# Expert loop of a two-block model: VectorE alone makes the low halves of the weight tiles, and the gated units are split ahead of them

## The chip, the core and the metric

The program runs on one core of one Trainium2 chip. The time is the device time of one execution in microseconds (us), as a median over runs. The core has five engines with queues of their own: TensorE (PE, with its weight loads shown apart as PEld), VectorE (DVE), ScalarE (ACT), GpSimd (POOL) and SyncE (SP), which only issues DMAs here. They meet at semaphores: an instruction waits until a counter has reached a value, and a finished instruction raises one.

## What is computed

Two models are applied in a row to 256 tokens of width 1024 in fp32: a first block of two layers (convolution and state-space mixers, adaptive norms, and a mixture of experts), and a second block of four layers with plain feed-forward parts. The part that the change touches is the mixture of experts of the first block, which runs once a layer:

```python
def hier_moe(h, p):            # top-1 expert group, then top-2 SwiGLU experts inside it
    ...
    def expert(acc, ew):
        wg, wu, wd, cw = ew
        hid = jax.nn.silu(t @ wg) * (t @ wu)
        return acc + (cw[:, None] * (hid @ wd)).astype(acc.dtype), None
    out, _ = lax.scan(expert, jnp.zeros(t.shape, jnp.float32),
                      (p["w_gate"], p["w_up"], p["w_down"], comb))
```

There are 16 experts with 256 hidden units each.

## The kernel before

**Three products for one.** Every large fp32 product is made of three products in a reduced fp32 format (`mm3`, lines 655 to 659): high part times high part, low part times high part, high part times low part. So each weight tile that a DMA brings into `ring` (four buffers of 128x2048) needs a high part, which ACT rounds off into one of two buffers `high` (`make_high`, L1212), and a low part, tile minus high part, written over the tile itself (`make_low`, L371). The down tiles (`dring`, 128x1024) have the same pair in L1218 (`make_down_high`) and L378 (`make_down_low`). `shared(c)` says for each tile whether its low part is cut in two: then DVE makes columns 0 to 1023 and POOL 1024 to 2047, with a semaphore each (`low_dve`, `low_pool`), and TensorE waits for both in `low_ready` (L355). Of the down tiles, DVE and POOL always make 512 columns each.

**The expert loop.** Tokens have been sorted into blocks of 128 rows, one block `b` for each expert, and each expert is two slices `j` of 128 hidden units. So a layer's loop has 16 blocks, 32 slices, in a hardware loop of four slices a turn. An even slice `j` and the odd one after it form a pair. The engines' queues, in the order of one slice (`one(j, g)` in each `experts`):

- TensorE: in an even slice turn the rows of the next block (L895, eight transposes); gate and up product of tile j+1, first half (12 matmuls of L657 to L659); turn the hidden units of slice j (L912, waits for `hid_raw`); second half of the product; the down product of slice j (six matmuls, waits for the down tile's low parts and for `hidden`). Each half of the gate and up product waits for the tile's low parts **and** for `x_split`, the low part of the block's rows. So the first product of a block, which TensorE makes in the odd slice before it, needs tile and rows of that block ready.
- ACT: SiLU of the gate (L1407, `gate_act`); high part of weight tile j+2 (L1212, 128x2048); high part of the turned hidden units (L1411, `hid_high`); in an even slice the high part of the next block's rows (L1389, two instructions); high part of down tile j+1 (L1218); in an odd slice, once the down product is done, copy the block's result out (L1398, two instructions) and store it (L1403).
- DVE: hidden units = SiLU times up (L1976, `hid_raw`); low part of weight tile j+2, its half (L371); low part of the hidden units (L1980, `hidden`); in an even slice the low part of the next block's rows (L1971, two instructions, then `x_split`); low part of down tile j+1, its half (L378).
- POOL: in an even slice the load of the rows of a later block (L540); its halves of weight tile j+2 (L371) and of down tile j+1 (L378).

Ahead of the loop stands the router (L1862 on), a chain of small DVE instructions; DVE and POOL make the low part of the layer's second expert tile just before it (`tiles(("rt", l))`). A second loop for experts with over 128 tokens (`over`) is skipped at run time here.

## Time and profile before

| | us |
|---|---|
| median of 3 runs | 2782.28 |
| lowest and highest of the 3 | 2775.22, 2788.04 |
| span of the profiled execution | 2783.9 |
| PE busy over the span | 2328.6 (84%) |
| DVE busy | 1625.2 (58%) |
| POOL busy | 1323.9 (48%) |
| ACT busy | 1104.4 (40%) |

The profiled execution is one execution, and its span stands 1.6 us above the median of the three runs. The two expert loops lie at about 524 to 712 us and at 1063 to 1260 us of it, some 385 us together. Busy times of the whole span mix stages with quite different limits, so the loops are read by themselves. In a timeline row the first number is the start in us from the span's start, the second the duration in us; a row "x2" is two instructions in a row; the bracket tells how long the engine had been idle and what ended that.

### The profile page before, as it was taken

The page shows a single profiled execution, that of the slowest core. Times are in us where ns is not written, and L with a number is a line of the kernel's source. Part 1 is how long each engine was busy: PE and PEld are TensorE (multiplying, and loading weights), DVE is VectorE, ACT ScalarE, POOL GpSimd, SP SyncE. Part 2 cuts the span into 40 slices and gives each one's busy share as a digit, 9 for nine tenths or more (in the row PEclk, how much of TensorE's full clock was granted, in tenths as well). Part 3 has the DMA queues.
Part 4 walks back from the last instruction along what each step waited for, and adds up shares of the span by engine and source line. Part 5 has one row for each costly group of instructions (what it writes and reads, how often), then busy time and mean ns, then how long its engine had stood idle before and what let it go on. Part 6 is the DMA issues. An engine that isn't in the chain of part 4 may idle for free.

```text
span 2783.9 us, 41385 instructions
## 1 busy us (share of the span) xinstructions
PE 2328.6 (84%) x15250; PEld 1960.5 (70%) x15250; DVE 1625.2 (58%) x2522; ACT 1104.4 (40%) x1581; POOL 1323.9 (48%) x744
## 2 busy tenths in 40 slices
PE   5998777788498767785999997768999799999998
PEld 2864545677385466674868995325899699887998
DVE  3488464477558545674247555996555755523654
ACT  3222533466433435764434442001443344444443
POOL 2320132588442336882654552874565256441553
PEclk7995888899797888997989998668999899999999
DMA  5258602699326037883405441001455244342442
GB/s 228 91 202 322 217 15 91 228 341 344 144 96 252 1 112 268 321 296 133 171 24 199 186 172 71 0 0 52 165 192 189 91 181 182 135 152 91 152 181 91
DMA packets 93047, 443.73 MB, mean 159 GB/s; under 512 B 9088, under 2 KB 25600, under 8 KB 56704
## 3 DMA queue, kind: packets, MB, share of 16 engines
q1 hardware_dynamic: 79104, 390.10, 38.6%
q0 software_dynamic: 8496, 31.99, 3.0%
q10 hardware_dynamic: 5328, 20.04, 1.8%
q8 instruction: 77, 1.26, 0.2%
q14 instruction: 42, 0.34, 0.0%
HBM read 401.20 MB, written 40.89 MB: 159 GB/s over the span
## 4 chain that ended last, share of the span: by engine, by line
PE 40%; DVE 5%; POOL 3%; ACT 2%; DVEq 2%; POOLq 1%; issue 1%; DMA 0%; ACTq 0%
PE bank L657 11%; PE bank L658 11%; PE bank L659 11%; POOL ring_halves L371 2%; PE bank L699 2%; ACT high L1212 1%; PE bank L1123 1%; POOLq L593 1%; DVEq L2179 1%; PE bank L1061 1%; DVE HT L1633 1%; POOLq L598 1%; PE bank L1038 1%; DVE rstd L1618 1%; PE bank L1051 1%
## 5 line engine op out<-in xcount | busy, mean ns | idle before, releaser
L371 POOL TENSOR_TENSOR ring_halves<-ring,high 128x1024 fp32r<-128x1024 f32 (+1 forms) x230 | 814.2, 3541 | 953.9 <-ACT high L1212 953.9
L657 PE MATMUL bank<-ssdb_halves,high 128*128 128x256 f32 (+1 forms) x2080 | 619.6, 298 | 65.8 <-DVE HT_halves L1627 34.8
L658 PE MATMUL bank<-HT_halves,high 128*128 128x256 f32 (+1 forms) x2096 | 627.4, 299 | 0.0
L659 PE MATMUL bank<-ssdb_halves,ring_halves 128*128 128x256 f32 (+1 forms) x2080 | 615.5, 296 | 0.0
L1212 ACT CAST high<-ring 128x2048 fp32r<-128x2048 f32 x230 | 438.0, 1906 | 89.7 <-PE bank L659 89.7
L657 PEld LDWEIGHTS bank<-ssdb_halves,high 128*128 128x128 f32 x2080 | 400.8, 193 | 90.5 <-issue 61.2
L371 DVE TENSOR_TENSOR ring_halves<-ring,high 128x1024 fp32r<-128x1024 f32 x200 | 279.5, 1398 | 248.0 <-ACT high L1212 247.9
L658 PEld LDWEIGHTS bank<-HT_halves,high 128*128 128x128 f32 x2096 | 402.6, 192 | 8.9
L659 PEld LDWEIGHTS bank<-ssdb_halves,ring_halves 128*128 128x128 f32 x2080 | 398.4, 192 | 9.6
L378 DVE TENSOR_TENSOR dring_halves<-dring,dhigh 128x512 fp32r<-128x512 f32 x152 | 309.6, 2037 | 53.1 <-ACT dhigh L1218 53.0
L378 POOL TENSOR_TENSOR dring_halves<-dring,dhigh 128x512 fp32r<-128x512 f32 x152 | 264.5, 1740 | 80.7 <-ACT dhigh L1218 80.6
L657 PE MATMUL bank<-border_halves,dhigh 128*128 128x256 f32 x704 | 197.5, 281 | 0.0
L659 PE MATMUL bank<-border_halves,dring_halves 128*128 128x256 f32 x704 | 197.3, 280 | 0.0
L658 PE MATMUL bank<-border_halves,dhigh 128*128 128x256 f32 x704 | 197.3, 280 | 0.0
L1218 ACT CAST dhigh<-dring 128x1024 fp32r<-128x1024 f32 x152 | 160.8, 1058 | 54.2 <-PE bank L659 54.1
L659 PE MATMUL bank<-high,HT_halves 128*128 128x256 f32 x640 | 182.0, 284 | 0.0
L1456 ACT ACTIVATE border<-bank 128x256 f32<-128x256 f32 x88 | 33.8, 384 | 365.0 <-PE bank L659 365.0
L657 PE MATMUL bank<-high,HT_halves 128*128 128x256 f32 x512 | 156.8, 306 | 18.0 <-POOL ring_halves L371 11.0
L2017 DVE TENSOR_TENSOR border<-border,bank 128x256 f32<-128x256 f32 x88 | 37.1, 422 | 213.9 <-ACT border L1456 213.1
L1123 PE MATMUL bank<-wide,zs_b 128*32 128x256 f32 x256 | 96.7, 547 | 62.5 <-DVE wide L2190 62.5
L658 PE MATMUL bank<-ring_halves,HT_halves 128*128 128x256 f32 x512 | 145.5, 284 | 0.0
L657 PEld LDWEIGHTS bank<-border_halves,dhigh 128*128 128x128 f32 x704 | 132.6, 188 | 0.1
(415 smaller groups left out, 4603.3 us busy)
## 6 DMA issues: line engine op xcount, KB each, us to landing
ring<-in_ffn SPq DMA_DIRECT2D x88, 1024.0 KB, 5.4
ring<-in_moe SPq DMA_DIRECT2D x64, 1024.0 KB, 7.3
ring<-in_ada SPq DMA_DIRECT2D x48, 1024.0 KB, 6.9
dring<-in_ffn_down SPq DMA_DIRECT2D x88, 512.0 KB, 3.6
dring<-in_moe_down SPq DMA_DIRECT2D x64, 512.0 KB, 4.6
ring<-in_foxin SPq DMA_DIRECT2D x24, 1024.0 KB, 4.8
ring<-in_win SPq DMA_DIRECT2D x22, 1024.0 KB, 4.8
zs_b<-x_slots POOLq DMA_DIRECT2D x32, 512.0 KB, 8.8
```

Of the source, the lines that this page charges most:

```text
L371: eng.tensor_tensor(low, w, h, ALU.subtract).then_inc(sem(f"low_{engine}"), 1)
L378: eng.tensor_tensor(low, w, h, ALU.subtract).then_inc(sem(f"down_low_{engine}"), 1)
L593: pool.drain()
L657: mm(o, a[0], b[0], start=first, stop=last and bool(kw), **kw)
L658: mm(o, a[0], b[1], start=False, stop=last and bool(kw), **kw)
L659: return mm(o, a[1], b[0], start=False, stop=last, **kw)
L699: i = mm(ps[7][:, 0:tok.stop - tok.start], k("mean1024"), sq[:, c, tok], start=c == 0, stop=c == KC - 1)
L1123: i = mm(y, cT[:, part, j, :], z, start=False, stop=n == 3, skip_group_check=True, tile_position=(0, q))
L1212: nc.scalar.copy(r(high[c % HIGH][:]), ring[t % RING][:]).then_inc(sem("high"), 1)
L1218: nc.scalar.copy(r(dhigh[d % HIGH][:]), dring[d % RING][:]).then_inc(sem("down_high"), 1)
L1456: act_fn(gact[:, j % 2, :], ps[4 + j % 2][:, 0:T], ACT.Silu).then_inc(sem("gate_act"), 1)
L2017: tt(hraw, gact[:, j % 2, :], ps[4 + j % 2][:, T:2 * T], ALU.mult)
```

## The change

Tiles are sorted into three kinds. `LOW_POOL` (win, wout): POOL alone, as before. `LOW_BOTH` (the feed-forward, attention and S5 weights): both engines, half each, as before. All others, which are the router's tile and the expert tiles (rt, moe, over), and the experts' down tiles: DVE alone, 2048 and 1024 columns in one instruction. `CUT[c]` is the column up to which DVE works, and `LOWS` and `DOWN_LOWS` count each engine's tiles so that the waits of TensorE name the right value. POOL's part of the expert loop keeps only the loads of rows. And in DVE's slice, the low part of the hidden units comes directly behind the product that makes them, ahead of the weight tile.

```diff
-WITH_DVE = ("rt", "moe", "over", "ffn", "foxin", "foxf", "foxout", "s5in", "glu")
+LOW_POOL = ("win", "wout")
+LOW_BOTH = ("ffn", "foxin", "foxf", "foxout", "s5in", "glu")
...
-            SHARED.append((SHARED[-1] if SHARED else 0) + (_n[0] in WITH_DVE))
+            CUT.append(0 if _n[0] in LOW_POOL else TILE // 2 if _n[0] in LOW_BOTH else TILE)
+            for _e, _own in (("dve", CUT[-1] > 0), ("pool", CUT[-1] < TILE)):
+                LOWS[_e].append((LOWS[_e][-1] if LOWS[_e] else 0) + _own)
...
         def low_ready(c, g=0):
 
-            if shared(c):
-                nc.tensor.wait_ge(sem("low_dve"), SHARED[c] + RING * g)
-            nc.tensor.wait_ge(sem("low_pool"), c + 1 + RING * g)
+            if CUT[c] > 0:
+                nc.tensor.wait_ge(sem("low_dve"), LOWS["dve"][c] + RING * g)
+            if CUT[c] < TILE:
+                nc.tensor.wait_ge(sem("low_pool"), LOWS["pool"][c] + RING * g)
...
         def make_low(eng, engine, c, g=0):
 
-            if engine == "dve" and not shared(c):
+            at_ = slice(0, CUT[c]) if engine == "dve" else slice(CUT[c], TILE)
+            if at_.start == at_.stop:
                 return
-            cut = TILE // 2 if shared(c) else 0
-            at_ = slice(0, cut) if engine == "dve" else slice(cut, TILE)
...
         def make_down_low(eng, engine, d, g=0):
-            at_ = slice(0, D // 2) if engine == "dve" else slice(D // 2, D)
+            at_ = slice(0, DOWN_CUT[d]) if engine == "dve" else slice(DOWN_CUT[d], D)
+            if at_.start == at_.stop:
+                return
...
                         rows(j // 2 + 2, g)
-                    if j + 2 < slices:
-                        make_low(pool, "pool", c0 + j + 2, g)
-                    if j + 1 < slices:
-                        make_down_low(pool, "pool", d0 + j + 1, g)
...
                     tt(hrows[:, j % 2, :], gact[:, j % 2, 0:P], ps[4 + j % 2][:, P:TCOLS], ALU.mult).then_inc(sem("hid_raw"), 1)
-                    if j + 2 < slices:
-                        make_low(dve, "dve", c0 + j + 2, g)
                     dve.wait_ge(sem("hid_high"), hid_high0 + j + 1 + RING * g)
                     tt(r(hid[:, j % 2, 1, 0:P]), ps[4 + j % 2][:, TCOLS:TCOLS + P], hid[:, j % 2, 0, 0:P], ALU.subtract)\
                         .then_inc(sem("hidden"), 1)
+                    if j + 2 < slices:
+                        make_low(dve, "dve", c0 + j + 2, g)
```

DVE's queue in an even slice of the expert loop, before. The names are output<-inputs; `ring_halves` is the tile's low part, `border_halves` the low part of the hidden units, `HT_halves` that of the rows, `dring_halves` that of the down tile.

```order
L1976 TENSOR_TENSOR border<-border,bank 128x128 [waits gate_act]
L369 REGISTER_ALU
L371 TENSOR_TENSOR ring_halves<-ring,high 128x1024 [waits high]
L1980 TENSOR_TENSOR border_halves<-bank,border_halves 128x128 [waits hid_high]
L1968 REGISTER_ALU
L1971 TENSOR_TENSOR HT_halves<-bank,HT_halves 128x512 [waits x_high]
L1971 TENSOR_TENSOR HT_halves<-bank,HT_halves 128x512
L376 REGISTER_ALU
L378 TENSOR_TENSOR dring_halves<-dring,dhigh 128x512 [waits down_high]
```

The same slice in the changed kernel, whose lines are numbered a little differently (L1974, L1976, L376, L1969 and L385 are what L1976, L1980, L371, L1971 and L378 were):

```order
L1974 TENSOR_TENSOR border<-border,bank 128x128 [waits gate_act]
L1976 TENSOR_TENSOR border_halves<-bank,border_halves 128x128 [waits hid_high]
L374 REGISTER_ALU
L376 TENSOR_TENSOR ring_halves<-ring,high 128x2048 [waits high]
L1966 REGISTER_ALU
L1969 TENSOR_TENSOR HT_halves<-bank,HT_halves 128x512 [waits x_high]
L1969 TENSOR_TENSOR HT_halves<-bank,HT_halves 128x512
L383 REGISTER_ALU
L385 TENSOR_TENSOR dring_halves<-dring,dhigh 128x1024 [waits down_high]
```

The split of the hidden units has moved ahead of the weight tile, and weight and down tile have doubled in columns; the rows' split stands behind the weight tile in both.

POOL's queue in the same even slice, before:

```order
L544 REGISTER_ALU
L540 ISA [waits x_turned]
L540 DMA zs_b<-x_slots 128x1024
L369 REGISTER_ALU
L371 TENSOR_TENSOR ring_halves<-ring,high 128x1024 [waits high]
L376 REGISTER_ALU
L378 TENSOR_TENSOR dring_halves<-dring,dhigh 128x512 [waits down_high]
```

And in the changed kernel, up to the end of the loop's turn:

```order
L551 REGISTER_ALU
L547 ISA [waits x_turned]
L547 DMA zs_b<-x_slots 128x1024
L393 REGISTER_ALU
L393 COMPARE_AND_BRANCH
```

Both low parts have left the queue, so a load of rows now waits for nothing but the buffer (`x_turned`) and the load before it.

## Rows read from the trace of the kernel before

**Rows 1.** Busy times by stretch: window, us, each engine (instructions), clock, DMA share, GB/s.
```profile
540.00:700.00 160.00, 135.62 (x915) 118.03 (x913) 119.98 (x132) 110.72 (x158) 139.60 (x66) 1.00 0.93 338
1075.00:1243.00 168.00, 134.93 (x915) 117.85 (x914) 118.53 (x130) 117.38 (x164) 138.97 (x66) 1.00 0.91 325
```

**Rows 2.** Waits from 540 to 700 us: who waited for whom, us, times, longest.
```profile
PE bank L657 <- DVE border_halves L1980: 16.3, 13, 1.3
...
PE bank L657 <- POOL ring_halves L371: 4.9, 12, 0.4
```

**Rows 3.** Timeline of TensorE over one pair, 606 to 620 us.
```profile
606.71 0.39 PE L659 MATMUL bank<-dhigh,border_halves 128*128 128x512 f32 x1
...
607.73 0.36 PE L657 MATMUL bank<-high,HT_halves 128*128 128x256 f32 x1
...
612.53 0.47 PE L657 MATMUL bank<-dhigh,border_halves 128*128 128x512 f32 x1 [1.25 <-DVE border_halves L1980]
...
614.57 0.38 PE L657 MATMUL bank<-high,HT_halves 128*128 128x256 f32 x1 [0.41 <-POOL ring_halves L371]
...
616.11 0.27 PE L912 MATMUL bank<-con,border 128*128 128x128 f32 x1
...
618.82 0.40 PE L659 MATMUL bank<-dhigh,border_halves 128*128 128x512 f32 x1
```

**Rows 4.** Timeline of ACT, the same pair.
```profile
607.14 1.08 ACT L1398 COPY ssdb<-bank 128x512 f32<-128x512 f32 x2 [1.62 <-PE bank L659]
...
609.02 1.90 ACT L1212 CAST high<-ring 128x2048 fp32r<-128x2048 f32 x1
610.82 0.27 ACT L1411 CAST border_halves<-bank 128x128 fp32r<-128x128 f32 x1
610.97 1.08 ACT L1389 CAST HT_halves<-bank 128x512 fp32r<-128x512 f32 x2
611.93 1.08 ACT L1218 CAST dhigh<-dring 128x1024 fp32r<-128x1024 f32 x1
...
613.04 1.93 ACT L1212 CAST high<-ring 128x2048 fp32r<-128x2048 f32 x1
```

**Rows 5.** Timeline of DVE, the same pair.
```profile
610.96 1.23 DVE L371 TENSOR_TENSOR ring_halves<-ring,high 128x1024 fp32r<-128x1024 f32 x1 [1.51 <-ACT high L1212]
612.10 0.28 DVE L1980 TENSOR_TENSOR border_halves<-bank,border_halves 128x128 fp32r<-128x128 f32 x1
612.30 1.28 DVE L1971 TENSOR_TENSOR HT_halves<-bank,HT_halves 128x512 fp32r<-128x512 f32 x2
613.50 1.50 DVE L378 TENSOR_TENSOR dring_halves<-dring,dhigh 128x512 fp32r<-128x512 f32 x1
614.92 0.28 DVE L1976 TENSOR_TENSOR border<-border,bank 128x128 f32<-128x128 f32 x1
```

**Rows 6.** Timeline of POOL, the same pair.
```profile
611.00 3.44 POOL L371 TENSOR_TENSOR ring_halves<-ring,high 128x1024 fp32r<-128x1024 f32 x1 [1.44 <-ACT high L1212]
```

**Rows 7.** Lines L371 and L378 on DVE, whole span: ns least/median/most.
```profile
L371 DVE TENSOR_TENSOR ring_halves<-ring,high x200: 1211/1226/3440, 434.3 to 2748.3; 128x1024 fp32r<-128x1024 f32 x100
...
L378 DVE TENSOR_TENSOR dring_halves<-dring,dhigh x152: 679/2306/2879, 503.1 to 2758.5; 128x512 fp32r<-128x512 f32 x152
```

**Rows 8.** Timelines of ACT and POOL, first pair of the first loop.
```profile
526.24 0.27 ACT L1411 CAST border_halves<-bank 128x128 fp32r<-128x128 f32 x1 [0.34 <-PE bank L912]
...
525.98 3.44 POOL L371 TENSOR_TENSOR ring_halves<-ring,high 128x1024 fp32r<-128x1024 f32 x1 [8.39 <-ACT high L1212]
```

**Rows 9.** Timeline of DVE in the routers of layer 0 and layer 1.
```profile
478.53 0.74 DVE L1874 TENSOR_TENSOR rt<-rt,rs 128x16 f32<-128x16 f32 x1
...
1027.17 0.20 DVE L1865 TENSOR_TENSOR rt<-bank,vec 128x40 f32<-128x40 f32 x1 [0.70 <-PE bank L735]
...
1027.68 1.02 DVE L1874 TENSOR_TENSOR rt<-rt,rs 128x8 f32<-128x8 f32 x1
```

**Rows 10.** Timeline of DVE, a pair of the second loop.
```profile
1089.19 0.29 DVE L1976 TENSOR_TENSOR border<-border,bank 128x128 f32<-128x128 f32 x1 [2.90 <-ACT border L1407]
```

More of the change, by code:

```diff
@@ L160 @@
 TILE_AT, SPLIT_AT, DOWN_AT = {}, {}, {}
-SPLIT, SHARED, DOWNS = [], [], 0
+SPLIT, CUT, DOWN_CUT, DOWNS = [], [], [], 0
+LOWS = {"dve": [], "pool": []}
+DOWN_LOWS = {"dve": [], "pool": []}
 _at = 0
@@ L171 @@
         DOWNS += _k
+        for _ in range(_k):
+            DOWN_CUT.append(D // 2 if _n[0] in LOW_BOTH else D)
+            for _e, _own in (("dve", True), ("pool", DOWN_CUT[-1] < D)):
+                DOWN_LOWS[_e].append((DOWN_LOWS[_e][-1] if DOWN_LOWS[_e] else 0) + _own)
     _at += _k
-def shared(c):
-    return SHARED[c] > (SHARED[c - 1] if c else 0)
 def program(nc, dram, out, known):
@@ L554, in experts @@
                     rows(b, 0)
-                if name[0] == "over":
-                    for a in range(2):
-                        make_low(pool, "pool", c0 + a)
-                make_down_low(pool, "pool", d0)
                 slices_loop(pool, slices, one)
@@ L567, in skip @@
                     pool.drain()
-                    pool.sem_inc(sem("low_pool"), OVER_SLICES)
-                    pool.sem_inc(sem("down_low_pool"), OVER_SLICES)
                 if_overflow(pool, l, lambda: experts(name, OVER, EXPERTS * P), skip)
@@ L917, in down @@
                         pe.wait_ge(sem("out_taken"), taken0 + b - 1 + RING // 2 * g)
-                    pe.wait_ge(sem("down_low_dve"), d + 1 + RING * g)
-                    pe.wait_ge(sem("down_low_pool"), d + 1 + RING * g)
+                    pe.wait_ge(sem("down_low_dve"), DOWN_LOWS["dve"][d] + RING * g)
+                    if DOWN_CUT[d] < D:
+                        pe.wait_ge(sem("down_low_pool"), DOWN_LOWS["pool"][d] + RING * g)
                     pe.wait_ge(sem("hidden"), hid0 + j + 1 + RING * g)
@@ L982, in down @@
                     d = d0 + j
-                    pe.wait_ge(sem("down_low_dve"), d + 1 + RING * g)
-                    pe.wait_ge(sem("down_low_pool"), d + 1 + RING * g)
+                    pe.wait_ge(sem("down_low_dve"), DOWN_LOWS["dve"][d] + RING * g)
+                    if DOWN_CUT[d] < D:
+                        pe.wait_ge(sem("down_low_pool"), DOWN_LOWS["pool"][d] + RING * g)
                     pe.wait_ge(sem("hidden"), hid0 + j + 1 + RING * g)
```

## The prediction, made before the run

> **What bounds the kernel now.** I read the stretches first, since the change touches only the two expert loops and the tiles just ahead of them. In both loops no engine is full: in the 160 us of the first one PE is busy 135.6, POOL 139.6, DVE 120.0 and ACT 110.7 us, at the full granted clock, with the DMA engines busy 0.93 of the time [rows 1]. So each pair of slices is a chain that goes round several engines, and what counts is its length. The waits say where TensorE stands still: 13 times for the low part of the hidden units (L1980), 16.3 us in all, and 12 times for POOL's half of the weight tile's low part (L371), 4.9 us [rows 2]. The change goes for both. Then I followed one pair through the timelines. The reader should lay rows 3 to 6 side by side:
>
> - TensorE ends an odd slice's down product at 607.10 (606.71 + 0.39) [rows 3]. ACT has waited for it: it copies the block out until 608.22, makes the gate's SiLU, rounds the next weight tile until 610.92, and rounds the turned hidden units until 611.09 [rows 4].
> - DVE takes its half of the weight tile at 610.96 and only then, at 612.10, the low part of the hidden units [rows 5]. TensorE starts the down product at 612.53 [rows 3].
> - POOL's half of the weight tile runs from 611.00 to 614.44 [rows 6], and TensorE starts the next block's product 0.13 us later, at 614.57 [rows 3]. From there it runs without a stop through the turn of the next hidden units (616.11) to the end of the odd down product, 618.82 + 0.40 = 619.22, which is 4.65 us [rows 3]. There the chain closes: 619.22 - 607.10 = 12.12 us for a pair.
>
> The link to see is that the wait for L1980 is **not** what sets the pair. The down product it starts ends near 614.2, and TensorE then waits 0.41 us for POOL's half in any case [rows 3]. An earlier L1980 alone would lengthen that second wait by what it takes off the first. The chain goes: odd down product, ACT until 610.92, POOL until 614.44, TensorE until 619.22. In the second loop the even slice starts later in some pairs (DVE idle 2.90 us before L1976), because of work on ACT ahead of this point [rows 10]. That lies before the first link and the change leaves it.
>
> **DVE's price for whole tiles.** The trace has no 2048-column subtraction on DVE. Undisturbed, 1024 columns take 1.21 us and 512 take 0.68 (least values) [rows 7], so a column costs 0.532/512 us = 1.04 ns, and 1024 more cost 1.06: 1.23 + 1.06 = 2.29 us for the weight tile and about 1.23 for the down tile. The next instruction starts 0.09 us before the end of one (610.96 + 1.23 against 612.10) [rows 5], so a tile takes 2.20 us of the queue and a down tile 1.14. Bounds: from below two 1024-column halves cannot cost less than their columns, 2.13 us; from above two whole instructions, 2.46. I take 2.29 because it carries one start only, as one instruction does.
>
> What POOL's absence gives back: 512 columns of down tile take 1.50 us beside POOL and end 0.56 us after POOL's 614.44, though 0.68 is enough alone [rows 5 to 7]. So DVE had waited for POOL's instruction to end. This loss goes, and the 1024-column down tile (1.14) is cheaper in the queue than the 512 columns were (614.92 - 613.50 = 1.42) [rows 5].
>
> **The even slice, step by step.** The high part of the hidden units is ready at 611.09 as before. DVE reacts in about 0.04 us (610.92 to 610.96) [rows 4, 5]:
>
> - L1980 from 611.13, 0.97 us earlier. It takes 0.20 us of the queue (612.10 to 612.30) [rows 5]. The down product starts at about 611.5 instead of 612.53 and ends near 613.2.
> - The whole weight tile from 611.33 to 613.62.
> - The rows' low parts (two L1971) from 611.33 + 2.20 = 613.53, and 1.28 us long [rows 5], until 614.81. Their high parts are ready at 612.05 [rows 4].
> - TensorE's next product needs the tile **and** the rows. The tile alone would let it go at 613.75; the rows let it go at 614.81 + 0.13 = 614.94. Before, the rows were done at 613.58 and nobody waited for them.
> - The down tile from 614.73 (its high part is ready at 613.01 [rows 4]), then L1976 of the odd slice from 615.87 to 616.15. TensorE asks for that at 616.11 + 0.37 = 616.48. It is covered, by 0.3 us.
>
> So the chain has 614.94 where it had 614.57: **0.37 us longer**. The two waits of TensorE become one, of about 1.7 us, for L1971.
>
> **The odd slice.** Here the reordering makes DVE wait for the hidden units before it starts its tile. L912 at 616.48, plus 0.27 on PE, 0.27 on ACT and two reactions, puts L1980 at 617.1 and the tile's end at 617.1 + 0.20 + 2.29 = 619.6; its high part is ready at 614.97 [rows 4]. TensorE wants it for the product after the row turn, at 607.73 + 12.12 + 0.37 = 620.22 [rows 3]. It is covered by 0.6 us. POOL keeps only loads of rows, which now go out as soon as their buffer is free; they stood behind two subtractions, so they can only be earlier. Their cost is nothing. Nothing is added to the queues of ACT and SP.
>
> **The sum.** In each layer 15 of 16 pairs have a next block and so this link. 28 of the 30 pairs cost 0.37: 10.4 us. In the first pair of a loop ACT's L1411 ends later, at 526.51, and DVE now waits for it: 526.55 + 0.20 + 2.20 + 1.28 + 0.13 = 530.36 against POOL's 525.98 + 3.44 + 0.13 = 529.55 [rows 8], 0.81 each, twice 1.6. Ahead of each loop the router's chain loses a wait for POOL: L1874 takes 0.74 and 1.02 us where a small instruction like L1865 takes 0.20 [rows 9]. The tile pass before it is 1.06 us longer, of which 0.70 lies in DVE's idle time [rows 9]. That leaves about -0.2 and -0.5, bounds +0.4 and -0.8 each: -0.8 together. Sum 10.4 + 1.6 - 0.8 = +11.2 us. Against the profiled execution 2783.9 + 11.2 = 2795.1. That execution stands 1.6 us above the median, so for the median 2782.3 + 11.2 = 2793.5 us, +0.40%.
>
> **Rivals.** *Faster, 2757.* The rows' split is not what TensorE waits for, and the tile is: TensorE goes at 613.75 instead of 614.57, -0.82 a pair, 30 times -24.6, with the router 2756.9. For it: L1980 is 0.97 us earlier, DVE's 2.29 for a whole tile beats POOL's 3.44 for a half, and DVE has idle time (120 of 160 us busy [rows 1]). Against it: the wait for `x_split` stands in the code, L1971 behind the tile, and even without it L1976 of the odd slice would be done at 616.15 only, while the product's first half would end near 615.3. So this needs DVE's later instructions to be shorter too. The Trainium skill (GPSIMD Engine Reference, "3.1 Elementwise — side-by-side cycle accounting") says that elementwise work belongs on VectorE, at about half GpSimd's time for the same columns, and by that rule alone the change should gain this 0.82 a pair; rows 6 and 7 agree on the rates, but not that rates decide.
>
> *Slower, 2799 and more.* The whole tile costs over 2.29 us on DVE. It has one place, between L1980 and L1971, and each 0.1 us above is 3 us in all. At the upper bound of 2.46 the pairs cost 0.54 (0.98 the first): 28 x 0.54 + 2 x 0.98 - 0.8 = +16.3, 2798.6. The half per cent is passed from 2.40 us on. Above 2.9 us the odd slice's cover of 0.6 us is gone as well and each pair pays twice. For it: nothing in this trace shows the size. Against it: 512 and 1024 columns lie on one line. The same page of the Trainium skill gives 2293 ns for a 2048-column fp32 tensor_tensor on VectorE; by that figure the sum stays what it is.
>
> *No effect, 2782.* If the pair is held elsewhere, DMA above all (0.93 of its time in the first loop [rows 1]), a longer chain on DVE fits into that slack. Against it: the view of waits for this stretch names no transfer.
>
> **How the numbers follow.** Forecast 0.70, faster rival 0.07, slower rival 0.18, no effect 0.05. The forecast's own range, by 2.13 to 2.40 us for the tile and the router's bounds, is 2788 to 2798. Changes of over 0.5% (13.9 us) are about what a measurement of this kernel can tell from none; 2796.2 lies inside the forecast's range, and three runs spread over 13 us, so I put a fifth of the forecast's chance beyond it. Faster 0.07; slower 0.18 + 0.15 = 0.33; within 0.60. The range goes from the no-effect case with some spread, 2779, to 2805, the slower rival at about 2.65 us a tile, and leaves out the faster rival and what is dearer still.
>
> **What would show each step.** In the profile after: DVE's 2048-column instruction at 2.3 us and L1971's start right behind it; L1980 about 2.0 us after L1976 in even slices instead of 2.9; TensorE's wait before the even down product down to some 0.3 us, its wait before the next block's first product up from 0.4 to 1.7 us and put down to L1971 instead of POOL; no wait of TensorE for the odd slice's L1976; pairs of about 12.5 us where they had 12.1, and 0.37 more for those with a longer start. It is wrong if that second wait is for the tile (then the rows' split is not late), if TensorE waits for the odd slice's hidden units, or if the two loops do not grow by some 6 us each.

## The result, and the profile after

| | before | after |
|---|---|---|
| median, us (14 runs each) | 2782.26 | 2791.47 |
| lowest and highest | 2770.74, 2789.38 | 2785.51, 2800.46 |
| ratio, 95% interval | | 1.0035 [1.0021, 1.0049] |
| span of the profiled execution | 2783.9 | 2791.1 |

The changed kernel is 9.2 us slower, 5.8 to 13.6 by the interval. The forecast was 2793.5 and +11.2. Line numbers move a little: L1976 to L1974 (hidden units), L1980 to L1976 (their low part), L371 to L376 (weight tile), L1971 to L1969 (rows), L378 to L385 (down tile), and on TensorE L657 to L659 become L653 to L655, L895 and L912 become L891 and L908.

The same view that [rows 2] shows, TensorE's waits from 540 to 700 us (what it waited for: us in all, times, longest), now reads:

```profile
PE bank L653 <- DVE HT_halves L1969: 21.7, 13, 1.7
PE bank L653 <- DVE border_halves L1976: 3.4, 12, 0.3
PE bank L908 <- DVE border L1974: 1.7, 5, 0.4
```

The wait for the hidden units has shrunk from 16.3 to 3.4 us, the wait for POOL is gone, and a wait for the low part of the **rows** has come, 21.7 us. Before, TensorE did not wait for the rows in this stretch. Two waits of 21.2 us have become two of 25.1 us.

One pair, in the timelines that [rows 3 to 5] show of before. TensorE (start, duration, what, how long it had been idle and for whom):

```profile
610.96 0.40 PE L655 MATMUL bank<-dhigh,border_halves 128*128 128x512 f32 x1
...
615.81 0.47 PE L653 MATMUL bank<-dhigh,border_halves 128*128 128x512 f32 x1 [0.28 <-DVE border_halves L1976]
...
619.11 0.39 PE L653 MATMUL bank<-high,HT_halves 128*128 128x256 f32 x1 [1.67 <-DVE HT_halves L1969]
...
620.65 0.27 PE L908 MATMUL bank<-con,border 128*128 128x128 f32 x1
```

ACT in the same pair:

```profile
611.39 1.08 ACT L1396 COPY ssdb<-bank 128x512 f32<-128x512 f32 x2 [1.62 <-PE bank L655]
...
613.10 0.28 ACT L1405 ACTIVATE border<-bank 128x128 f32<-128x128 f32 x1 [0.63 <-ACT ssdb L1396]
613.28 1.89 ACT L1210 CAST high<-ring 128x2048 fp32r<-128x2048 f32 x1
615.07 0.27 ACT L1409 CAST border_halves<-bank 128x128 fp32r<-128x128 f32 x1
615.23 1.09 ACT L1387 CAST HT_halves<-bank 128x512 fp32r<-128x512 f32 x2
```

DVE, the odd slice before it and then the pair's even slice:

```profile
608.86 0.29 DVE L1976 TENSOR_TENSOR border_halves<-bank,border_halves 128x128 fp32r<-128x128 f32 x1 [0.88 <-ACT border_halves L1409]
609.07 2.28 DVE L376 TENSOR_TENSOR ring_halves<-ring,high 128x2048 fp32r<-128x2048 f32 x1
...
613.41 0.29 DVE L1974 TENSOR_TENSOR border<-border,bank 128x128 f32<-128x128 f32 x1 [0.93 <-ACT border L1405]
615.37 0.29 DVE L1976 TENSOR_TENSOR border_halves<-bank,border_halves 128x128 fp32r<-128x128 f32 x1 [1.67 <-ACT border_halves L1409]
615.58 2.28 DVE L376 TENSOR_TENSOR ring_halves<-ring,high 128x2048 fp32r<-128x2048 f32 x1
617.78 1.28 DVE L1969 TENSOR_TENSOR HT_halves<-bank,HT_halves 128x512 fp32r<-128x512 f32 x2
618.98 1.21 DVE L385 TENSOR_TENSOR dring_halves<-dring,dhigh 128x1024 fp32r<-128x1024 f32 x1
620.11 0.28 DVE L1974 TENSOR_TENSOR border<-border,bank 128x128 f32<-128x128 f32 x1
```

Read them as one chain. The odd down product ends at 611.36. ACT copies the block out, then makes the SiLU, the high part of the tile and, until 615.34, that of the hidden units. DVE makes the hidden units' low part at 615.37, the whole tile until 617.86, the rows until 619.06. TensorE starts at 619.11. The start before it was at 606.71, so a pair takes 12.40 us.

How the loops grew can be read from the low part of the hidden units, which each of a loop's 32 slices has once (least, median and most ns, then the first and the last start), before and then after, first loop and then second:

```profile
L1980 DVE TENSOR_TENSOR border_halves<-bank,border_halves x32: 276/282/294, 527.1 to 710.5; 128x128 fp32r<-128x128 f32 x32
L1980 DVE TENSOR_TENSOR border_halves<-bank,border_halves x32: 277/282/291, 1066.2 to 1258.9; 128x128 fp32r<-128x128 f32 x32
L1976 DVE TENSOR_TENSOR border_halves<-bank,border_halves x32: 290/292/294, 526.6 to 718.9; 128x128 fp32r<-128x128 f32 x32
L1976 DVE TENSOR_TENSOR border_halves<-bank,border_halves x32: 290/292/294, 1076.3 to 1274.6; 128x128 fp32r<-128x128 f32 x32
```

From first to last start 183.4 and 192.7 us before, 192.3 and 198.3 after. The first of these starts came earlier in its slice, which this measure counts as loop; from the first hidden units (L1976 before, L1974 after) to the same end the loops grew by 8.2 and 5.1 us.

One thing in the first loop was not in the forecast. The busy time of the engines by stretch (length, then PE, PEld, DVE, ACT, POOL with their instructions, granted clock, share and GB/s of DMA) shows TensorE at half clock, that is at 1.2 GHz, twice:

```profile
540.00:700.00 160.00, 132.57 (x888) 115.96 (x887) 114.69 (x128) 106.02 (x151) 5.82 (x11) 0.99 0.89 331
...
545.00:548.00 3.00, 3.00 (x15) 2.88 (x15) 2.69 (x3) 1.21 (x2) 0.00 (x0) 0.62 0.92 388
...
705.00:708.00 3.00, 1.25 (x10) 1.26 (x10) 2.96 (x5) 1.80 (x2) 0.00 (x0) 0.95 0.00 0
708.00:711.00 3.00, 3.00 (x16) 3.00 (x15) 1.52 (x2) 1.21 (x2) 0.00 (x0) 0.50 0.00 0
```

The fall near 543.8 follows TensorE's wait for the rows of 1.74 us, the one near 707.7 its wait of 1.75 us; matmuls of 256 columns take 0.41 us in it where they take 0.28 elsewhere. Each of the two places lasts some 3.4 us. The pair around the first takes 13.92 us instead of 12.40, and the one around the second, which is the last pair of the loop, 12.82 where the last pair of the second loop, at full clock, takes 11.31: 1.5 us each.

### The profile page after: what moved, and what is told of

The parts are those of the page before. It is cut to its first block, busy times and chain, and to the rows that moved or that the text cites. A ratio compares the mean times of both kernels' runs of the same rounds, so it can differ in the third digit from the quotient of the medians.

```text
span 2791.1 us, 41139 instructions
## 1 busy us (share of the span) xinstructions
PE 2328.0 (83%) x15250; PEld 1959.9 (70%) x15250; DVE 1625.0 (58%) x2522; ACT 1104.6 (40%) x1581; POOL 992.2 (36%) x614
## 4 chain that ended last, share of the span: by engine, by line
PE 40%; DVE 5%; POOL 3%; ACT 2%; DVEq 2%; issue 1%; POOLq 1%; DMA 0%; ACTq 0%
PE bank L653 11%; PE bank L654 11%; PE bank L655 11%; POOL ring_halves L376 2%; PE bank L695 2%; ACT high L1210 1%; PE bank L1121 1%; DVEq L2177 1%; DVE HT L1631 1%; PE bank L1059 1%; DVE rstd L1616 1%; DVE wide L2178 1%; PE bank L1036 1%; PE bank L1049 1%; PE bank L1105 1%
## 5 line engine op out<-in xcount | busy, mean ns | idle before, releaser
L376 POOL TENSOR_TENSOR ring_halves<-ring,high 128x1024 fp32r<-128x1024 f32 (+1 forms) x164 | 589.6, 3597 | 818.8 <-ACT high L1210 818.8
L653 PE MATMUL bank<-ssdb_halves,high 128*128 128x256 f32 (+1 forms) x2080 | 618.3, 297 | 65.9 <-DVE HT_halves L1625 34.7
L655 PE MATMUL bank<-ssdb_halves,ring_halves 128*128 128x256 f32 (+1 forms) x2080 | 613.9, 295 | 0.0
L653 PEld LDWEIGHTS bank<-ssdb_halves,high 128*128 128x128 f32 x2080 | 399.1, 192 | 91.1 <-issue 62.8
L376 DVE TENSOR_TENSOR ring_halves<-ring,high 128x1024 fp32r<-128x1024 f32 (+1 forms) x200 | 323.5, 1618 | 202.6 <-ACT high L1210 202.5
L655 PEld LDWEIGHTS bank<-ssdb_halves,ring_halves 128*128 128x128 f32 x2080 | 396.6, 191 | 9.7
L385 DVE TENSOR_TENSOR dring_halves<-dring,dhigh 128x512 fp32r<-128x512 f32 (+1 forms) x152 | 269.2, 1771 | 46.3 <-ACT dhigh L1216 40.1
L653 PE MATMUL bank<-high,HT_halves 128*128 128x256 f32 x512 | 158.4, 309 | 54.7 <-DVE HT_halves L1969 54.6
L653 PE MATMUL bank<-border_halves,dhigh 128*128 128x256 f32 x704 | 197.5, 281 | 0.0
L655 PE MATMUL bank<-border_halves,dring_halves 128*128 128x256 f32 x704 | 197.3, 280 | 0.0
L655 PE MATMUL bank<-high,HT_halves 128*128 128x256 f32 x640 | 183.6, 287 | 0.0
L385 POOL TENSOR_TENSOR dring_halves<-dring,dhigh 128x512 fp32r<-128x512 f32 x88 | 154.4, 1754 | 75.2 <-ACT dhigh L1216 75.2
L653 PEld LDWEIGHTS bank<-high,HT_halves 128*128 128x128 f32 x512 | 99.6, 195 | 68.9 <-DVE HT_halves L1969 54.2
```

Source lines behind the costliest of these rows:

```text
L376: eng.tensor_tensor(low, w, h, ALU.subtract).then_inc(sem(f"low_{engine}"), 1)
L385: eng.tensor_tensor(low, w, h, ALU.subtract).then_inc(sem(f"down_low_{engine}"), 1)
L653: mm(o, a[0], b[0], start=first, stop=last and bool(kw), **kw)
L655: return mm(o, a[1], b[0], start=False, stop=last, **kw)
```

## The experiments

My theory: after the change the chain goes through DVE's hidden units, tile and rows; taking the tiles from POOL and reordering are only nearly neutral together. Rivals: each part by itself is near neutral, as engines have spare time; or the pair is held by the transfers; or the granted clock makes the loss. Each median stands beside that of the kernel before, measured along with it. "Loops" is the measure of the rows just shown, first to last start of the hidden units' low part; "pairs" is the distance of such starts in even slices.

### 1. The order alone

The kernel before, with DVE's order of the changed kernel; POOL still makes its halves.

```diff
-                    if j + 2 < slices:
-                        make_low(dve, "dve", c0 + j + 2, g)
                     dve.wait_ge(sem("hid_high"), ...)
                     tt(...).then_inc(sem("hidden"), 1)
+                    if j + 2 < slices:
+                        make_low(dve, "dve", c0 + j + 2, g)
```

> The reordering alone: in the kernel before, DVE makes the low part of the hidden units (L1980) ahead of its half of the weight tile; both engines keep their halves. My theory (what counts is when tile AND rows are ready, and an instruction with two operands in SBUF makes the other engine wait for its whole length): POOL now starts first and alone, at 611.00 in the pair of the rows, and is done about 1.1 us earlier than its 3.44; DVE waits for it, makes its half until about 614.5, and the rows' split behind it ends near 615.7, so TensorE resumes 1.1 us later than before: pairs of 13.2 to 13.4 us, +34 us in all, about 2816 (2800 to 2825). Rival (the early L1980 is the gain and the takeover costs something): 2750 to 2782, at most the time before.

Measured: 2905.5 us against 2786.9, ratio 1.0429 [1.0390, 1.0467]; loops 255.3 and 245.2. The direction was right, the size far off. POOL and DVE in one pair:

```profile
539.53 2.39 POOL L371 TENSOR_TENSOR ring_halves<-ring,high 128x1024 fp32r<-128x1024 f32 x1 [3.12 <-ACT high L1212]
541.88 2.25 POOL L378 TENSOR_TENSOR dring_halves<-dring,dhigh 128x512 fp32r<-128x512 f32 x1
544.09 2.37 POOL L371 TENSOR_TENSOR ring_halves<-ring,high 128x1024 fp32r<-128x1024 f32 x1
```

```profile
539.64 0.29 DVE L1978 TENSOR_TENSOR border_halves<-bank,border_halves 128x128 fp32r<-128x128 f32 x1 [1.67 <-ACT border_halves L1411]
539.85 3.15 DVE L371 TENSOR_TENSOR ring_halves<-ring,high 128x1024 fp32r<-128x1024 f32 x1
542.92 1.28 DVE L1971 TENSOR_TENSOR HT_halves<-bank,HT_halves 128x512 fp32r<-128x512 f32 x2
544.12 2.88 DVE L378 TENSOR_TENSOR dring_halves<-dring,dhigh 128x512 fp32r<-128x512 f32 x1
546.93 0.28 DVE L1976 TENSOR_TENSOR border<-border,bank 128x128 f32<-128x128 f32 x1
```

Now POOL begins first, and DVE's half of the tile ends only 1.08 us after POOL's (541.92 to 543.00): 3.15 us for work that takes 1.21 undisturbed. DVE is held by the whole of POOL's instruction. It happens a second time with the down tile, 2.88 us, behind POOL's tile for the odd slice, and that I had not counted. It makes the odd slice's hidden units late, so TensorE waits for them as well (second line; its waits from 560 to 690 us):

```profile
PE bank L657 <- DVE HT_halves L1971: 20.3, 8, 2.5
PE bank L912 <- DVE border L1976: 8.8, 11, 1.2
```

That still does not make 119 us. The rest is the clock: in the first loop the first pair, at full clock, takes 14.2 us, the others about 17, and the granted clock is 0.79 over most of it. In the second loop the pairs from 1191 to 1222 us run at full clock and take 14.9 without a table load (experiment 9 has that load) and 16.4 with one, where those at half clock with a table load take up to 18.8. So the two holds cost some 2.7 us a pair against 12.2 before, over twice the 1.1 that I expected, and the clock comes on top. The first loop:

```profile
560.00:690.00 130.00, 99.70 (x527) 85.82 (x528) 84.18 (x78) 61.03 (x88) 68.69 (x39) 0.79 0.71 241
```

### 2. The takeover alone

The changed kernel with DVE's old order: tile, then hidden units.

```diff
+                    if j + 2 < slices:
+                        make_low(dve, "dve", c0 + j + 2, g)
                     dve.wait_ge(sem("hid_high"), ...)
                     tt(...).then_inc(sem("hidden"), 1)
-                    if j + 2 < slices:
-                        make_low(dve, "dve", c0 + j + 2, g)
```

> The takeover alone: DVE makes whole weight and down tiles, and L1980 stays behind the weight tile. My theory: L1980 ends near 613.4 instead of 612.4, the down product ends near 615.2, the rows' split is done before that, so TensorE is held by its own late down product, +0.67 us, and in the odd slice the hidden units come behind a 2.2 us tile, about +0.2 more: 0.7 to 0.9 us a pair against before, +20 to +26 us, about 2802 to 2808, so slower than the full change. Rival (the order is worth nothing, the takeover is the whole effect): the time of the full change, +9 to +11 us.

Measured: 2826.7 us against 2786.9, ratio 1.0161 [1.0121, 1.0201]; loops 202.1 and 209.9. Pairs at full clock take 13.08 and 13.30 us in turn, 0.96 more than before, a little over the 0.7 to 0.9 expected. The wait for the hidden units is back, and larger, since a tile of 2.29 us now stands before them:

```profile
PE bank L653 <- DVE border_halves L1978: 24.4, 14, 2.3
```

In ten places of the two loops the clock falls to 0.5 for some 3.4 us and the pair takes about 14.0, or 15.6 with a table load (experiment 9). With the first experiment this settles that neither part is neutral:

| ratio to the kernel before | old order | new order |
|---|---|---|
| DVE and POOL, half each | 1 | 1.0429 |
| DVE alone | 1.0161 | 1.0035 |

Whoever costs the two parts one at a time and adds, gets 5.9% by the ratios, or 158 us by the medians (118.6 and 39.8); together they cost 9. Half clock is a part of both single losses.

### 3. The rows ahead of the tile

If TensorE waits for the rows, should they not be made first? The changed kernel, with the rows' low part ahead of the tile; only the tile is moved.

```diff
-                    if j + 2 < slices:
-                        make_low(dve, "dve", c0 + j + 2, g)
                     if j % 2 == 0 and j // 2 + 1 < blocks:
                         split_rows(j // 2 + 1, g)
+                    if j + 2 < slices:
+                        make_low(dve, "dve", c0 + j + 2, g)
```

> The changed kernel with the rows' split (two L1969) moved ahead of the weight tile in even slices. My theory: TensorE needs both, whichever comes last; the rows' high parts are ready only at 612.05, so DVE idles 0.65 to 0.7 us and then does the same work: TensorE resumes 0.6 to 0.75 us later than in the changed kernel, and now for the tile. Pairs of about 13.05 us, +18 to +22 us over the changed kernel, 2810 to 2814. Rival (only the rows' split holds TensorE): the rows are ready about 1.4 us earlier, so 0.4 to 0.8 us a pair less than the changed kernel, 2767 to 2780.

Measured: 2836.0 us against 2786.9, ratio 1.0196 [1.0147, 1.0246]; loops 205.5 and 226.9. TensorE now waits for the tile:

```profile
PE bank L653 <- DVE ring_halves L376: 25.2, 10, 2.5
```

The rows' high part is the later one: in the pair shown above ACT ends it at 616.32 and the tile's at 615.17, while DVE is free for the next step at 615.58. So this order leaves DVE idle for some 0.8 us and then has the same two pieces to do. Pairs at full clock take 13.24 and 13.49 us, against some 13.05 expected; in three pairs of the first loop and eleven of the second the clock fell, and these take up to 16.3, a table load among it. That is the part of the miss that the next experiments look at.

### 4. The same with TensorE kept busy

Experiment 3, and behind the even down product 14 small products of zeros in bf16 into an unused corner of PSUM. They change no value and fill part of TensorE's wait.

```diff
+                    if j % 2 == 0:
+                        for _ in range(14):
+                            mm(ps[4][:, TCOLS + P:], zeros[:, 0:P], zeros[:, 0:P], start=True, stop=True)
```

> The kernel with the rows' split first (e3), and 14 small products of zeros into an unused corner of a PSUM bank, which nothing reads, in TensorE's wait behind the even down product. In e3 the granted clock fell to half for 3.4 us in 3 places of the first loop and in 11 of the second, and pairs with such a place were 1.3 to 1.6 us longer. The wait there is 2.5 us, the fillers take about 1.6. Theory (the chain gives 13.25 us a pair, and the rest of e3's loss is the clock, which falls because TensorE stands still): no half clock inside the loops, pairs of 13.2 to 13.5 and 14.8 with a table load, about 18 us less than e3, 2815 to 2820. Rival (the long pairs have another cause, or the clock falls for the long transfers of the other engines): no change, 2836, or slower by the fillers.

Measured: 2818.6 us against 2779.8, ratio 1.0137 [1.0099, 1.0175]; loops 202.1 and 211.4, the second 15.5 us shorter. The second loop without the fill and with it:

```profile
1090.00:1290.00 200.00, 152.12 (x925) 135.04 (x923) 118.15 (x131) 117.82 (x164) 6.33 (x12) 0.91 0.74 271
```

```profile
1090.00:1290.00 200.00, 160.00 (x1205) 140.76 (x1204) 128.72 (x144) 127.89 (x179) 6.33 (x12) 1.00 0.77 278
```

The granted clock goes from 0.91 to 1.00, and pairs at 13.24 and 13.48 stay what they were at full clock. So in experiment 3 the clock was a cost of its own on top of the chain.

### 5. The changed kernel, filled

The same with nine products on the changed kernel.

> The changed kernel with 9 such fillers in TensorE's wait behind the even down product (1.7 us there, fillers about 1.0). In the changed kernel's profile the clock fell for 3.4 us in two places of the first loop, 1.5 us each, and in none of the second. Theory: no such place, all pairs 12.4 to 12.7 (14.0 with a table load), the loops 3 us shorter together; the time 2785 to 2790, too little to be told from the changed kernel by the time alone. Rival: the long pairs stay.

Measured: 2789.8 us against 2779.8, ratio 1.0037 [1.0015, 1.0059]; loops 189.5 and 198.6. No half clock in either loop, and the pair that had taken 13.92 us takes 12.40. In the profiled executions this gives back 2.8 us in the first loop. The ratio is the changed kernel's 1.0035 all the same, with an interval of 0.22% to either side: what the clock costs the changed kernel in its other executions is not settled. That it is not the whole of the loss is: the profiled execution of this kernel has no half clock in the loops, and the kernel is slower than the one before by 0.15% at least.

### 6. Half of the rows' low part left out

Only a test of the term: the second of the two row instructions is left out, and the products of chunks 4 to 7 take the high part where the low part stood. TensorE's work is the same, DVE's is 0.60 us less.

```diff
-                    for n in range(2):
+                    for n in range(1):
                         hi, lo = ...
                         i = tt(r(lo), ps[6 + n][:], hi, ALU.subtract)
```

> The changed kernel without the second of the two instructions that split the rows (chunks 4 to 7 use the high part in place of the low part, so the output differs; TensorE's work is unchanged). It takes 0.60 us of DVE's queue away between the weight tile and TensorE's start. My theory: every pair with a next block is 0.55 to 0.6 us shorter than in the changed kernel, 30 times, -17 us: about 2774. Rival (the tile, or TensorE's clock, or transfers hold the pair): no more than 5 us less than the changed kernel, 2786 to 2791.

Measured: 2770.6 us against 2786.9, ratio 0.9957 [0.9931, 0.9983]; loops 180.2 and 189.3, pairs 11.80 and 12.04. The pair loses exactly the 0.60 us that DVE lost. So the rows' low part is on the chain with its full length, and TensorE's wait for it has become 1.1 us:

```profile
PE bank L653 <- DVE HT_halves L1969: 11.8, 11, 1.1
```

This rules out the transfers as what holds the pair, and the "no effect" rival with them.

### 7. The block's result taken out of the chain

The chain's next link is ACT: copy and store of the finished block stand ahead of the next SiLU (611.39 to 613.10 above). The changed kernel, with both moved to the end of the next even slice and the last one behind the loop.

```diff
-                    if j % 2:
-                        store(j // 2, g)
+                    if j % 2 == 0 and (j or not isinstance(g, int)):
+                        store(j // 2 - 1, g)
...
-                slices_loop(act, slices, one, 0 if taken0 else 1)
+                slices_loop(act, slices, one, 2)
+                store(blocks - 1, 0)
```

> The changed kernel, with ACT's copy and store of a finished block moved from the end of the odd slice to the end of the next even slice (and two turns of ACT's loop written out, as its first store comes late). My theory (a pair is a chain whose first link is the wait of ACT for the odd down product): that link goes, ACT makes the SiLU of the even slice as soon as its product is done, and a pair falls to TensorE's own work, 2 x 4.65 + 0.8 = 10.1 us, unless the transfers hold it: 338 GB/s at 0.93 busy is 363 at most, and 4.19 MB a pair take 11.5 us then. 0.9 to 2.4 us a pair less, and the reloads of ACT's table in the second loop (about 1.55 us in 7 turns) go too: -38 to -80 us against the changed kernel, 2710 to 2753. Rival (DVE, which now makes all low parts, is the bound): no gain beyond the table loads, 2780.

Measured: 2748.0 us against 2787.4, ratio 0.9867 [0.9835, 0.9900]; loops 170.3 and 170.3, pairs 11.14. Together the loops are 50 us shorter than in the changed kernel. Part of the gain in the second loop has another cause, the subject of experiment 9.

### 8. The same on the kernel before

> The same move of ACT's store in the kernel before, where POOL and DVE share the low parts. Theory: the same link goes, so it gains too; but here POOL is busy 139.6 of 160 us, which is 10.6 us a pair of 12.1, so POOL can become the bound at 10.6 plus the waits for each other. Expected 2715 to 2760, and the difference to the late store in the changed kernel tells what the takeover is worth once ACT's link is gone: the changed kernel 0 to 20 us faster. Rival: both the same as without the move but for the table loads, 2772.

Measured: 2763.2 us against 2787.4, ratio 0.9909 [0.9873, 0.9945]; loops 174.6 and 175.3, pairs 11.55; just above the expected range. What TensorE waits for now, with ACT's link gone:

```profile
PE bank L657 <- DVE border_halves L1981: 13.4, 11, 1.3
PE bank L657 <- POOL ring_halves L371: 2.2, 11, 0.2
```

Against experiment 7 the change under study is worth 15 us here by the medians (2763.2 - 2748.0), with the other sign. The size is loose: these are medians of five and four runs whose spreads just meet, and the loops of the two profiled executions differ by 9.3 us. Whether it gains depends on what stands around it.

### 9. A turn of ACT's loop written out

In the second loop every other pair is longer, before and after [rows 10]. ACT shows why (of the changed kernel):

```profile
1097.71 0.59 ACT L1396 COPY ssdb<-bank 128x512 f32<-128x512 f32 x1
...
1099.30 1.28 ACT L1405 ACT_TABLE_LOAD   x1 [0.99 <-ACT ssdb L1396]
1100.59 0.28 ACT L1405 ACTIVATE border<-bank 128x128 f32<-128x128 f32 x1
```

At the start of each turn of the hardware loop ACT loads its function table again, 1.28 us. In the first layer the first turn is written out ahead of the loop and no such load is there. The changed kernel, with that done in both layers:

```diff
-                slices_loop(act, slices, one, 0 if taken0 else 1)
+                slices_loop(act, slices, one, 1)
```

> The changed kernel with the first turn of ACT's second expert loop written out, as it is in the first loop. It should take the reload of ACT's table out of the 7 turns of that loop: pairs that begin a turn fall from 14.0 to about 12.6 us, -10 us, 2781. It tells how much of the late store's gain is the table's. If the reload is not on the chain, no change, 2791.

Measured: 2781.0 us against 2787.4, ratio 0.9987 [0.9964, 1.0011]; loops 190.7 and 189.4, the second 8.9 us shorter, its pairs 12.47 and 12.64, no table load inside. This is why the second loop is 9 us longer before, and 6 after, where the first has the two places at half clock. It has nothing to do with the change.

### 10. Order by parity

The experiments say what each slice needs. In an even slice the rows are last and the tile must be early; in an odd slice there are no rows, and the hidden units come first without harm. After experiment 7 there is room for it: in its even slices DVE stands idle for the hidden units' high part, though ACT has long made the tile's, and TensorE then waits for the rows (DVE's timeline, then TensorE's waits from 560 to 690 us, both of experiment 7):

```profile
613.80 0.29 DVE L1977 TENSOR_TENSOR border_halves<-bank,border_halves 128x128 fp32r<-128x128 f32 x1 [1.43 <-ACT border_halves L1409]
PE bank L653 <- DVE HT_halves L1970: 15.0, 12, 1.3
```

Without the late store the two high parts are ready at almost the same time (615.17 and 615.34 in the pair of the changed kernel), so this idle time isn't there. This run is experiment 7, with the tile ahead of the hidden units in even slices and behind them in odd ones:

```diff
+                    if j % 2 == 0 and j + 2 < slices:
+                        make_low(dve, "dve", c0 + j + 2, g)
                     dve.wait_ge(sem("hid_high"), ...)
                     tt(...).then_inc(sem("hidden"), 1)
-                    if j + 2 < slices:
+                    if j % 2 and j + 2 < slices:
                         make_low(dve, "dve", c0 + j + 2, g)
```

> The late store (e5) with DVE's order by slice: in even slices the whole weight tile ahead of the low part of the hidden units, in odd slices behind it. With the late store the even tile's high part is ready long before the hidden units, and DVE idled 1.4 us there, while TensorE waited 1.2 us for the rows' split that comes behind the tile. Theory (order pays where it fills DVE's idle time and costs where it does not): TensorE's wait of 1.2 us goes, pairs of 11.14 fall towards TensorE's own 10.1, down to what the transfers allow, so by 0.5 to 1.1 us, -15 to -33 us against e5: 2715 to 2733. Rival (e5 is at the limit of the transfers, busy 0.93 at 351 GB/s): 2744 to 2750, no change.

Measured: 2724.6 us against 2779.8, ratio 0.9789 [0.9750, 0.9829]; loops 160.8 and 160.3, pairs 10.58 and 10.60. It is faster than both kernels, 2.1% below the one before. Against experiment 7 the loops are 19.5 us shorter. The order by parity without the late store was not run. TensorE's waits, and the busy times from 560 to 690 and from 560 to 665 us:

```profile
PE bank L653 <- DVE border_halves L1979: 6.7, 14, 0.9
```

```profile
560.00:690.00 130.00, 122.41 (x840) 110.27 (x841) 106.03 (x124) 99.57 (x146) 4.77 (x9) 1.00 0.91 359
560.00:665.00 105.00, 100.02 (x694) 90.73 (x695) 87.50 (x101) 82.43 (x119) 4.77 (x9) 1.00 1.00 396
```

The wait for the rows is gone. TensorE is busy 94% of the first stretch, and ACT now twice waits for a weight tile's transfer, 0.8 us in all. The last 25 us have few transfers left; up to 665 us the DMA engines are busy all the time, at 396 GB/s. So the loop is close both to TensorE's own work and to its transfers. Which of the two would bound it next, no run here settles.

## Why the prediction was right

**The chain and its new end: right.** DVE from the hidden units' high part to the end of the rows was forecast as 3.72 us (611.09 to 614.81); it is 615.34 to 619.06, 3.72. The whole tile takes 2.28 us (2.29 forecast, from two smaller sizes), 2.20 in the queue; with that the slower rival falls, which needed a dearer tile. L1976 starts 1.96 us after the hidden units of the even slice (615.37 against 613.41; 2.0 forecast). TensorE's wait before the even down product is 0.28 us (0.3 forecast), the next one 1.67 and for the rows (1.7 forecast). Experiment 6 shows that the rows' instructions are on the path with their full length; experiment 3 swaps the two, and TensorE then waits for the tile, later still. The faster rival fails by the same fact: DVE is the faster engine for a tile, but the tile is not what TensorE waits for. One reading beside that rival was off: rows 6 and 7 do not agree with half the time for the same columns, since 3.44 against 1.23 us is 2.8 times. Only experiment 1, with 2.37 against 1.21, gives 2.0 times. Nothing in the sum rests on it.

**The size of the link: a little high.** Forecast 0.37 us a pair, measured 12.40 - 12.11 = 0.29, and the same 0.29 to 0.30 for the pairs with the longer start. The step that was off is the last reaction: TensorE started 0.05 us after DVE's rows (619.06 to 619.11), and the sum had borrowed 0.13 from POOL's instruction [rows 3, 6]. Over 28 pairs that is 2.1 us: 8.3 instead of 10.4. The first pairs cost the 0.81 forecast, within 0.1 (rows done 530.33, forecast 530.23).

**The odd slice: right.** The tile is done at 611.35 and TensorE uses it at 611.99, so 0.64 us of cover where 0.6 was forecast. The hidden units are done at 620.39 and turned at 620.65, 0.26 where 0.3 was forecast. TensorE's five waits for L1974, 1.7 us, are the longer starts of every other pair and stand in before as well.

**The router: right in kind.** The small instruction that took 0.74 and 1.02 us [rows 9] takes 0.17 both times, so the wait for POOL is gone. The 0.8 us net is too little to be read off by itself.

**The clock: the step that was missing.** The prediction took TensorE "at the full granted clock" from the stretch of before and never asked what longer single waits do to it. In the profiled execution after it cost 2 x 1.5 = 3.0 us. It is not the same in each execution: the first loop of experiment 9 is that of the changed kernel, and its profile has one such place and not two. By this profile the sum is 8.3 + 1.6 - 0.8 + 3.0 = 12.1 us; the loops show 8.2 + 5.1 = 13.3 without the router; the medians 9.2, with an interval that holds both. Two misses of 2 and 3 us of opposite sign stand in a forecast that came out 2 us high, so that the number came this close is in part luck; the mechanism is not. In the loops these few us can be told apart; in the medians they can't. Nor do the spans help: the part behind the second loop, which no kernel here changes, varies by 17 us between profiled executions.

In the expectations the same omission was dear. For experiments 1, 2 and 3 I worked out pairs at full clock. For the last two they came within 0.2 us, and most of what was missed was pairs at half clock; for the first I had also missed that DVE is held by POOL twice in a pair and not once, which made its pairs at full clock 14.2 to 14.9 us instead of the 13.2 to 13.4 expected.

## What to carry to other kernels

In a ring of engines, count at each join which of the inputs comes last, and move an instruction forward only if what then stands behind it is not the later input: here the two halves of the edit alone cost 1.6% and 4.3%, and together 0.35%. A tile order that serves two kinds of slices badly in one queue may serve both if it is chosen by kind, and work that only drains a result (ACT's copy and store) does not belong ahead of the next block's first link. These two gave the 2.1%, with the table load out of the second loop, which was worth 8.9 us in experiment 9. When an estimate lengthens a single wait of TensorE, ask for the granted clock of the stretch too.

## What the runs showed of the hardware

- **TensorE's clock.** With waits of 1.25 and 0.41 us a pair there was no half clock in the loops; with one of 1.67 us, two places, and one in experiment 9; with one of up to 2.5 us, fourteen in experiment 3. Each of these places is some 3.4 us at 0.5, and costs 1.3 to 1.6 us. Where nine or 14 small products filled the wait, there was none, and the second loop of experiment 3 fell by 15.5 us.
- **DVE beside POOL.** In experiment 1 DVE's instructions with both inputs in SBUF were held until POOL's, begun before them, ended: 3.15 us where 1.21 is undisturbed. The rows' two instructions, with one input in PSUM, take 1.28 us beside a busy POOL (542.92) and 1.28 beside an idle one (617.78).
- **POOL's own price.** The 1024 columns that took 3.44 us in before [rows 6] take 2.37 to 2.39 in experiment 1, where POOL starts first. The difference of 1.07 us is about the length of the instruction that DVE had begun 0.04 us earlier there, so the 3.44 held a wait for DVE, and the 2.4 is the work.
- **The transfers.** In the fastest kernel the DMA engines moved 396 GB/s over 105 us of the loop (560 to 665 us) on this one core, busy all the time, where TensorE was busy 95%. The share alone is a poor measure of the room left: before, it was 0.93 at 338 GB/s [rows 1], and the 363 GB/s at most, which the expectation of experiment 7 made of these two, was no limit.
